# Block 2's feed-forwards as two plain slices and three seven-product pairs, and a rearranged way into block 1's pairs

## The reference

```python
u = jax.nn.relu(rms_norm(h, ff_norm[i]) @ w_ff1[i])      # 256 x 1024 @ 1024 x 4096
h = h + (u * u) @ w_ff2[i]                               # 256 x 4096 @ 4096 x 1024
g = jax.nn.sigmoid(rms_norm(h, ple_norm[i]) @ w_ple_gate[i])
h = h + g * (p[i] @ w_ple_proj[i])
```

## Time and profile before

| | |
|---|---|
| median of three runs | 1946.69 us (1946.23 to 1947.9) |
| profiled execution | 1946.73 us, its span 1944.7 us |
| TensorE busy | 1896.4 us, 98% of the span |
| VectorE, ScalarE busy | 72%, 51% |
| mean granted clock of TensorE | 0.996 |
| block 1's feed-forwards begin near | 8, 454, 640 and 1081 us |
| block 2's feed-forwards | about 1389 to 1573 us and 1727 to 1911 us |

### The profile page before, as it was taken

How to read it: one execution, slowest core, us unless ns; L and a number is a source line. 1 busy time by engine, 2 the same in 40 slices (tenths; PEclk the granted TensorE clock), 3 DMA queues, 4 the chain that set the end, 5 groups by cost and what they waited for, 6 DMA issues and landing times.

```text
span 1944.7 us, 23187 instructions
## 1 busy us (share of the span) xinstructions
PE 1896.4 (98%) x9016; PEld 1553.2 (80%) x9016; DVE 1405.9 (72%) x1599; ACT 1000.5 (51%) x1203; POOL 108.4 (6%) x176
## 2 busy tenths in 40 slices
PE   8999999999999999999999999989999999999999
PEld 6788788887788778878888778877788887778887
DVE  6887766778887888777667988878755466775545
ACT  4555444544555455543554455557544355654443
POOL 2001100000000000110000000011000000100000
PEclk9999999999999999999999999999999999999999
DMA  9764554447764666565345766365465555346542
GB/s 345 230 217 167 199 191 173 148 156 260 230 222 145 226 216 216 187 215 196 131 173 165 246 216 217 125 170 174 136 227 173 172 179 178 120 152 211 182 163 87
DMA packets 177729, 366.39 MB, mean 188 GB/s; under 512 B 7408, under 2 KB 51360, under 8 KB 176096
## 3 DMA queue, kind: packets, MB, share of 16 engines
q1 hardware_dynamic: 170512, 334.85, 49.9%
q0 software_dynamic: 7120, 30.21, 6.0%
HBM read 351.39 MB, written 1.05 MB: 181 GB/s over the span
## 4 chain that ended last, share of the span: by engine, by line
PE 82%; DVE 11%; ACT 3%; DVEq 2%; DMA 1%; issue 1%; SPq 0%; ACTq 0%
PE acc L834 49%; PE aux L834 16%; PE aux L1110 10%; DVE w_low L2504 3%; DVE w_low L2673 2%; DVE buf_v L2678 1%; PE aux L849 1%; DMA buf_q<-ffn_w 1%; ACT w_high L1942 1%; PE aux L945 1%; PE aux L1242 1%; DVEq L2556 1%; DVE xT_low L2510 1%; PE aux L1073 1%; DVE mix_param L2711 0%
## 5 line engine op out<-in xcount | busy, mean ns | idle before, releaser
L2504 DVE TENSOR_TENSOR w_low<-w_raw,w_high 128x2048 fp32r<-128x2048 f32 (+2 forms) x268 | 604.2, 2267 | 208.5 <-ACT w_high L1844 205.0
L1844 ACT CAST w_high<-w_raw 128x2048 fp32r<-128x2048 f32 (+2 forms) x268 | 502.9, 1893 | 249.4 <-PE acc L834 207.7
L834 PE MATMUL acc<-w_high,yT_high 128*128 128x512 f32 (+1 forms) x836 | 331.6, 397 | 3.0 <-DVE yT_low L2688 2.5
L834 PE MATMUL acc<-w_high,yT_low 128*128 128x512 f32 (+1 forms) x836 | 326.0, 390 | 0.0
L834 PE MATMUL acc<-w_low,yT_high 128*128 128x512 f32 (+1 forms) x836 | 325.6, 389 | 0.0
L834 PE MATMUL acc<-w_high,xT_high 128*128 128x512 f32 (+2 forms) x752 | 298.0, 396 | 7.0 <-DVE xT_low L2510 4.5
L834 PE MATMUL acc<-w_high,xT_low 128*128 128x512 f32 (+2 forms) x752 | 291.4, 388 | 0.0
L834 PE MATMUL acc<-w_low,xT_high 128*128 128x512 f32 (+2 forms) x752 | 291.1, 387 | 0.0
L834 PE MATMUL aux<-w_high,xT_high 128*128 128x512 f32 x576 | 229.9, 399 | 7.2 <-DVE w_low L2504 4.5
L834 PE MATMUL aux<-w_high,xT_low 128*128 128x512 f32 x576 | 225.3, 391 | 0.0
L834 PE MATMUL aux<-w_low,xT_high 128*128 128x512 f32 x576 | 224.7, 390 | 0.0
(11 more groups left out here) (385 smaller groups left out, 2329.1 us busy)
## 6 DMA issues: line engine op xcount, KB each, us to landing
w_raw<-w_ff SPq DMA_DIRECT2D x64, 1024.0 KB
w_raw<-w_in SPq DMA_DIRECT2D x52, 1024.0 KB
w_raw<-ffn_w SPq DMA_DIRECT2D x44, 1024.0 KB
w_raw<-ffn_w SPq DMA_DIRECT2D x78, 512.0 KB
w_raw<-w_branch SPq DMA_DIRECT2D x16, 1024.0 KB
buf_v<-ffn_w SPq DMA_DIRECT2D x12, 1024.0 KB, 9.1
buf_u<-ffn_w SPq DMA_DIRECT2D x12, 1024.0 KB, 6.0
buf_q<-ffn_w SPq DMA_DIRECT2D x12, 1024.0 KB, 6.9
```

Source lines behind the costliest of these rows:

```text
L834: last = nc.tensor.matmul(dst, lhs[:, kt, tok], rhs(j), start=(kt == k_first and q == 0), stop=(kt == k_last and q == 2))
L1844: nc.scalar.copy(whi[:, s, 0:size], raw[:, s, 0:size]).then_inc(slot_hi[s], 1)
L2504: V.tensor_tensor(wlo[:, s, 0:size], raw[:, s, 0:size], cast(whi[:, s, 0:size]), ALU.subtract)\
```

## The change

**Block 2.** The loops go. Each feed-forward is straight code over 41 units (`ffn2_units`): slices 0 and 1 plain, slices 2 to 7 as three pairs of seven block products each. The weights' blocks go through the same four buffers as in block 1, each pair's sum w by a DMA from POOL. Relu and square of a pair are one VectorE operation on three of the four parts (`squared_relu`) and a relu on ScalarE with a multiply on VectorE for the fourth. A pair's down products (four units, e_0 to e_3) are placed between the next pair's products; behind the first pair's products stands slice 1's down part. The pair's values are transposed in two groups (`quad_T`) into all four banks of `aux`. The tile of p moves from `buf_q` to a part of `ln_param`.

**Block 1.** In the way into the first pair of each feed-forward, two of the four whole values of x are no longer made from high and low parts: one is read from the bank of the transposes, the other from a copy of its bank by ScalarE. The low part of b11 is no longer made by VectorE: ScalarE writes the negated high part (the scaled copy writes fp32r) and a DMA issued by POOL adds B11 to it. VectorE waits for that DMA before it adds B12 to B11. ScalarE does the high part of h1_0 before the first activation, and the second slice's activation and transposed values before the high part of b21; a one-element activation stands ahead of everything.

The core of the diff, in the order: units, SP, POOL (block 1, block 2), TensorE block 2, ScalarE block 1, VectorE block 2, VectorE block 1. ScalarE's part of block 2 follows the same order as VectorE's: high parts one to two units ahead, the copies of the bank between them.

```diff
+    order = ["h0_0", "h0_1", "h1_0", "h1_1", "d0_0", "d0_1",
+             "b11_0", "b21_0", "v_0", "x_0", "d1_0", "w_0", "y_0", "b22_0", "d1_1"]
+    done = ["h0_0", "h1_0", "d0_0", "d0_1",
+            "b11_0", "b21_0", "v_0", "x_0", "w_0", "d1_0", "y_0", "b22_0", "d1_1"]
+    for q in range(1, QUADS2):
+        e = [f"e{q - 1}_{k}" for k in range(4)]
+        order += [f"b11_{q}", f"b21_{q}", f"v_{q}", f"x_{q}", e[0], f"w_{q}", e[1], f"y_{q}", e[2], f"b22_{q}", e[3]]
+        done += [f"b11_{q}", f"b21_{q}", f"v_{q}", f"x_{q}", e[0], f"w_{q}", e[1], f"y_{q}", e[2], f"b22_{q}", e[3]]
+    e = [f"e{QUADS2 - 1}_{k}" for k in range(4)]
+    return order + e, {name: k for k, name in enumerate(done + e[0:3])}
...
+    def quad_load2(i, q, r):
+        freed = {R11: "y", R21: "y", R12: "w", R22: "b22"}[r]
+        if q > 0:
+            s, n = ffn2_unit(i, f"{freed}_{q - 1}")
+            sp.wait_ge(slot_lo[s], n + 2)
+        else:
+            sp.wait_ge(form_done, FORMS * (2 * DEPTH + i) + 1)
...
+    def ffn2(i):
+        for name in ("h1_0", "h1_1", "d0_0", "d0_1"):
+            load_ffn2(i, name)
+        for r in (R11, R21, R12, R22):
+            quad_load2(i, 0, r)
+        for name in ("d1_0", "e0_0", "e0_1", "d1_1"):
+            load_ffn2(i, name)
+        for r in (R12, R21, R11, R22):
+            quad_load2(i, 1, r)
+        for name in ("e0_2", "e0_3", "e1_0", "e1_1"):
+            load_ffn2(i, name)
+        for r in (R12, R21, R11, R22):
+            quad_load2(i, 2, r)
+        for name in ("e1_2", "e1_3", "e2_0", "e2_1", "e2_2", "e2_3"):
+            load_ffn2(i, name)
...
+        n = 2 * l + which
+        s = FFN_UNIT["b11_0"][0]
+        pool.wait_ge(b11_neg, n + 1)
+        pool.dma_start(wlo[:, s, :], sum_raw[R11], accum_op=ALU.add).then_inc(b11_sum, 16)
+        pool.wait_ge(b11_sum, 16 * n + 16)
+        pool.sem_inc(slot_lo[s], 1)
...
+                for q in range(QUADS2):
+                    k = quads2_before(i, q)
+                    pool.wait_ge(sum_done, 3 * k + 1)
+                    pool.wait_ge(r_full[R22], 16 * k + 16)
+                    pool.dma_start(sum_raw[R12], sum_raw[R22], accum_op=ALU.add).then_inc(w_sum, 16)
...
+        for j in range(2):
+            hidden_unit(0, 1, j)
         for j in range(2):
             hidden_unit(1, 0, j)
+        plain_T(0)
+        for j in range(2):
             hidden_unit(1, 1, j)
         for p in range(2):
             pe.wait_ge(acc_read[p], n_acc[p].k + 1)
+        down("d0_0")
+        down("d0_1")
+        plain_T(1)
+        for q in range(QUADS2):
+            terms, combined = quad_act2(i, q), 3 * quads2_before(i, q)
+            fill = [f"e{q - 1}_{k}" for k in range(4)]
+            pe.wait_ge(aux_read[1], aux0[1] + PLAIN2 + q + 1)
+            block_product(ffn2_unit(i, f"b11_{q}"), 1, *x_part(0, 0), True)
+            pe.wait_ge(aux_read[0], aux0[0] + PLAIN2 + q + 1)
+            block_product(ffn2_unit(i, f"b21_{q}"), 0, *x_part(0, 1), True)
+            pe.wait_ge(aux_read[3], aux0[3] + PLAIN2 + q + 1)
+            block_product(ffn2_unit(i, f"v_{q}"), 3, *form(f, 0), True)
+            pe.wait_ge(quad_act, terms + 1)
+            block_product(ffn2_unit(i, f"x_{q}"), 1, *form(f, 2), False)
+            if q == 0:
+                down_part("d1_0", 0)
+            else:
+                down(fill[0])
+            pe.wait_ge(quad_act, terms + 2)
+            block_product(ffn2_unit(i, f"w_{q}"), 1, *form(f, 1), False)
+            if q == 0:
+                down_part("d1_0", 1).then_inc(unit_used, 1)
+            else:
+                down(fill[1])
+            pe.wait_ge(quad_act, terms + 3)
+            block_product(ffn2_unit(i, f"y_{q}"), 1, *x_part(1, 1), False)
+            if q > 0:
+                down(fill[2])
+            pe.wait_ge(quad_read, combined + 2)
+            block_product(ffn2_unit(i, f"b22_{q}"), 3, *form(f, 3), False)
+            late = "d1_1" if q == 0 else fill[3]
+            down_part(late, 0)
+            quad_T(q, 0)
+            down_part(late, 1).then_inc(unit_used, 1)
+            quad_T(q, 1)
...
+        nc.scalar.activation(nz[:, 0:1], ident[:, 0:1], ACT.Silu)
+        tile1()
+        aux0[2:] = [n_aux[2].k, n_aux[3].k]
+        high_plain("h1_0")
+        activate(0, 0)
+        act.wait_ge(aux_read[3], aux0[3] + 1)
+        nc.scalar.copy(quarter[1], aux[:, 3, :]).then_inc(form_in, 1)
+        high_plain("h1_1")
+        activate(0, 1)
         high_plain("d0")
         loaded(0, R11)
         high_sum("b11", 0, R11)
+        nc.scalar.activation(wlo[:, FFN_UNIT["b11_0"][0], :], sum_raw[R11], ACT.Copy, scale=-1.0)\
+            .then_inc(b11_neg, 1)
         for n in range(FORMS):
             act.wait_ge(form_done, FORMS * (2 * l + which) + n + 1)
             nc.scalar.copy(form_h[:, n, :, :].rearrange("p k c -> p (k c)"), quarter[FORM_AT[n]])\
                 .then_inc(form_hi, 1)
-        used("h1_0")
+        activate(1, 0)
+        plain_high_T(0)
         loaded(0, R21)
         high_sum("b21", 0, R21)
-        activate(1, 0)
-        plain_high_T(0)
         activate(1, 1)
         summed(0, 1)
         high_sum("v", 0, R11)
...
+        def squared_relu(term, combined):
+            dve.wait_ge(quad_read, combined)
+            V.scalar_tensor_tensor(term, term, 0.0, term, ALU.max, ALU.mult).then_inc(h_ready, 1)
...
         combine(1, 0, 1, ALU.subtract)
         dve.drain()
         combine(0, 2, 0, ALU.subtract)
+        low_plain("h1_1")
+        multiply(0, 1)
+        combine(2, 1, 2, ALU.subtract)
+        dve.drain()
+        combine(3, 3, 2, ALU.add)
+        low_plain("d0_0")
+        low_plain("d0_1")
+        for n in range(FORMS):
+            form_low(f, n)
+        for b in (2, 3):
+            dve.wait_ge(aux_full[b], n_aux[b].k + 1)
+        multiply(1, 0)
+        plain_low_T(0)
+        low_sum("b11", 0, R11)
+        multiply(1, 1)
+        add_to(0, R11, R12)
+        low_sum("b21", 0, R21)
+        low_sum("v", 0, R11)
+        plain_low_T(1)
+        for q in range(QUADS2):
+            combined, terms = 3 * quads2_before(i, q), quad_act2(i, q)
+            fill = [f"e{q - 1}_{k}" for k in range(4)]
+            add_to(q, R11, R22)
+            low_sum("x", q, R11)
+            low_plain("d1_0" if q == 0 else fill[0])
+            add_to(q, R11, R21)
+            low_sum("w", q, R12)
+            if q > 0:
+                low_plain(fill[1])
+            dve.wait_ge(quad_act, terms + 1)
+            dve.wait_ge(unit_used, ffn2_done(i, f"b21_{q}"))
+            V.tensor_tensor(term1, aux[:, 0, :], term1, ALU.add).then_inc(quad_read, 1)
+            low_sum("y", q, R11)
+            squared_relu(term1, combined + 1)
+            if q > 0:
+                low_plain(fill[2])
+            dve.wait_ge(quad_act, terms + 3)
+            V.tensor_tensor(term3, aux[:, 3, :], term3, ALU.subtract).then_inc(quad_read, 1)
+            low_sum("b22", q, R22)
+            squared_relu(term3, combined + 2)
+            low_plain("d1_1" if q == 0 else fill[3])
+            dve.wait_ge(quad_act, terms + 4)
+            V.tensor_tensor(silu1, silu1, aux[:, 1, :], ALU.mult).then_inc(h_ready, 1)
+            if q + 1 < QUADS2:
+                low_sum("b11", q + 1, R11)
+                add_to(q + 1, R11, R12)
+                low_sum("b21", q + 1, R21)
+            else:
+                tail = [f"e{q}_{k}" for k in range(4)]
+                low_plain(tail[0])
+                low_plain(tail[1])
+            dve.wait_ge(unit_used, ffn2_done(i, f"b22_{q}"))
+            V.tensor_tensor(term2, aux[:, 3, :], term2, ALU.subtract).then_inc(quad_read, 1)
+            squared_relu(term2, combined + 3)
+            if q + 1 < QUADS2:
+                low_sum("v", q + 1, R11)
+            else:
+                low_plain(tail[2])
+            quad_low_T(q, 0)
+            quad_low_T(q, 1)
...
+        dve.drain()
+        h0 = n_hi.k
+        low_plain("h1_0")
+        multiply(0, 0)
+        whole(0, 0, 2)
+        whole(0, 1, 3)
+        dve.wait_ge(form_in, 2 * l + which + 1)
+        V.tensor_tensor(quarter[1], aux[:, 2, :], quarter[1], ALU.subtract).then_inc(form_done, 1)
+        dve.drain()
+        V.tensor_tensor(quarter[0], quarter[2], aux[:, 2, :], ALU.subtract).then_inc(form_done, 1)
         multiply(0, 1)
         low_plain("h1_1")
         combine(2, 1, 2, ALU.subtract)
         dve.drain()
         combine(3, 3, 2, ALU.add)
         low_plain("d0")
-        form_low(0)
+        form_low(2 * l + which, 0)
         dve.wait_ge(aux_full[2], n_aux[2].k + 1)
         multiply(1, 0)
         plain_low_T(0)
         for n in range(1, FORMS):
-            form_low(n)
-        low_sum("b11", 0, R11)
+            form_low(2 * l + which, n)
         multiply(1, 1)
+        s, n = ffn_unit(l, which, "b11_0")
+        dve.wait_ge(slot_lo[s], n + 2)
         add_to(0, R11, R12)
         low_sum("b21", 0, R21)
```

(66 more changed lines are left out.)

529 lines of the change are left out of this document (279 added, 250 removed).

## The result

The changed kernel takes 1974.58 us (median of 4 runs, 1974.33 to 1974.68), the kernel before 1947.3 on the same chip: 1.0139 times, interval 1.0127 to 1.0152. The forecast was 1952, with a range from 1936 to 1962. The direction was right, the size was not: 27 us were lost, not 5. The page of after, beside the earlier trace rows: 72 products fewer on TensorE, 90 us more of VectorE, and TensorE's part in the chain that ended last down from 82% to 69%.

The account below looks back on a forecast made before the run. TensorE, busy for 98% of the span, was taken as the bound. Saved products -16.4, first-pair waits +24.2, clock +1.6 and block 1's lead-in -3.6 gave +5.8 on 1946.73: 1952 us, range 1936 to 1962.

Parts of the forecast that it names:

- Block 2's saving (-8.2 a feed-forward): Block 2, TensorE: 732 products instead of 768 per feed-forward, 36 x 0.227 = 8.2 us less, twice: -16.4 us.
- the waits of the first pair: Block 2's first pair: TensorE waits at h1_0, h1_1, d0, w_0, term2's transposes, next b11; 12.1 us per feed-forward, bounds 8.2 to 15.
- In the later pairs ... I charge nothing there: Block 2 after the first pair: VectorE is done 3 us before term2 is wanted, so no waits charged, 0 us.
- sign of being wrong, waits in the middle pairs: Block 2: waits in the middle pairs would make VectorE the bound at each pair and the time worse than the range.
- The clock, 0.8 a feed-forward: Block 2, behind the 4.7 us wait: TensorE's granted clock falls, costing 0.8 us per feed-forward (0 to 3.4), +1.6 in all.
- Block 1's lead-in, -3.6: Block 1's first pairs: b11's DMA sum lands in 8.0 us, first sum 1.6 us earlier; -3.6 us over four feed-forwards.
- the bound given (+4): Upper end of the range for block 1's lead-in, from -8.6 to +4 us.
- The zero for the first feed-forward: Block 1's first feed-forward: loads fill the queues, a DMA may take 12 us; from -1.8 to +1.2, taken as 0.

Follow-up runs that it names:

- the short sum: Changed kernel with e1_0 and e1_1 loads behind the third pair's block loads; VectorE's first sum for block 2's second pair cut to 16 of 2048 columns: 1956.22 us.
- the fill: 17 unread products on TensorE ahead of term2's wait in block 2's first pair: changed kernel 1975.61 us; with e1_0, e1_1 loads behind block loads 1964.53 us.
- the reordered kernel: Changed kernel with old block 1 lead-in, block 2's VectorE list in TensorE's order (second order tried), e1_0 and e1_1 loads behind third pair's blocks: 1948.07 us.
- the loads held: Kernel before with block 1's new lead-in and DMA sum; SP holds loads of d2 and d3 until b11's DMA sum has landed: 1942.61 us.
- without the DMA: Kernel before with block 1's new lead-in, but b11's low part made by VectorE, no negated copy or adding DMA: 1938.22 us.
- the early loads alone: Changed kernel with loads of e1_0 and e1_1 moved behind the third pair's block loads on SP: 1962.42 us.
- the other two orders: Changed kernel, term2 and square before next b11, sum, b21: 1967.4 us; reordered block 2 plus DMA-free block 1 lead-in, multiply before h1_1's low part: 1941.89 us.

## Why the prediction was wrong

**Block 2's saving (-8.2 a feed-forward) and the waits of the first pair: right.** Forecast 0.4, 2.3, 1.3, 1.2, 4.7 and 2.2; measured 0.22, 1.87, 0.73, 1.02, 4.22 and 0.83 in the first feed-forward. That is 8.9 us for 12.1, with every wait in its place, and the short sum showed for the longest of them that VectorE's operations set it. The forecast was out by most at the last, 2.2 for 0.83. With the clock kept up by the fill that wait is 1.71 us; in the changed kernel the transposes ahead of it run at 1.2 GHz (1.97 us for 1.09), and 0.88 us of the wait go by in them.

**"In the later pairs ... I charge nothing there": failed.** The waits were 2.6 us in the first and 4.8 in the second feed-forward (0.86 + 1.71, 3.07 + 1.68). The step looked at VectorE's slack of 3 us and took B11's landing to be what it was in the first pair. It did not put the third pair's B11, which is wanted at the end of the second, in its place in SP's queue, behind four loads of 1 MB: it landed in 14.9 us instead of 8.6. Moving two of them took those waits away, and 10.6 us off the two feed-forwards. The prediction's sign of being wrong, waits in the middle pairs, came true, but behind a late load and not for the amount of VectorE's work.

**The clock, 0.8 a feed-forward, "between 0 and 3.4": mis-sized.** It is 3.2 in the first. And in the changed kernel it can't be added as a term of its own: with the clock up, the second pair's wait in the first feed-forward was 3.35 us and not 0.86, and the time between the pairs was the same.

**A term was left out: the restart.** The first feed-forward is 9.5 us longer. -8.2 for the products, +11.6 for nine waits and +3.2 for the clock leave 2.9. The 0.27 us beyond the idle time, which the reordered kernel shows at each wait, make 2.4 of it. The prediction counted the idle times alone.

**Block 1's lead-in, -3.6: failed at the landing.** It was taken at 8.0 us "with the loads of the pair beside it", from twelve sums of which none had a load issued in the 5 us ahead of it or before its landing; it was 9.6 to 11.5, and with the loads held 7.0 in the second and fourth feed-forward. The part loses 4.9 us by itself (2.3 to 6.0), about the bound given (+4). The rest of the step held: VectorE is free at 480.58 - 1.87 = 478.7, the 1.1 us wait is gone, and TensorE waits at x_0. The zero for the first feed-forward was wrong as well: +1.8 in the changed kernel, -5.35 without the DMA.

**Sum.** Forecast 24.2 - 16.4 + 1.6 - 3.6 = +5.8. Measured on the two profiled executions: block 2 +9.5 and +12.2, ahead of it +6.4, between its feed-forwards -0.3: +27.8. Of the 22 us between the two, 10 are what stands ahead of block 2, where -3.6 had been forecast. 7.3 are the second pairs' waits, and 7 must be taken off, by which the first pairs' waits came out shorter. That leaves about 12 us for the clock and the restarts beyond the 1.6 forecast, the largest single miss. In the first feed-forward they are the 3.2 and 2.9 above; the second has 7.3 us beyond its waits of 13.1, and how that divides was not taken apart.

## What to carry to other kernels

Where an engine at 98% is relieved by work on one at 72%, go through the stretch in which the second is full, operation by operation. The sum cut out there gave back its own length and more. Reordering helped (block 2's two feed-forwards took 413.9 us in the second order and 425.0 with the early loads alone) but did not bring block 2 below the 413.9 of the kernel before; in the other two orders the wait came back elsewhere. Take the landing of a load or a DMA sum from a row with the same queue in front of it and the same loads beside it, and for each pair anew. And test the parts of a change one by one: here the part that was meant as a helper had the gain, as soon as its DMA was taken out again or kept clear of the loads.

## What the runs showed that I had not expected

A 1 MB adding DMA on GpSimd's queue landed in 7.0 us in two of three feed-forwards with no load issued beside it (9.0 in the other, not explained), and in 9.6 to 11.5 us with two loads issued within some 2 us of it. A wait of TensorE cost 0.27 us over its idle time, so that a wait of 0.2 us cost more than twice what it shows. Keeping TensorE's clock at 2.4 GHz through a wait of 4 us by filling it gained 2.4 us in one feed-forward and nothing in the kernel.
